# Up projection of the second block as seven products of halves, tokens stationary

## The reference, cut to what matters

```python
h = x + merged @ w_out
z = rmsnorm(h, norm_mlp) @ w_mlp_in              # 256 x 1024 by 1024 x 4096
return h + jnp.square(jax.nn.relu(z)) @ w_mlp_out   # 256 x 4096 by 4096 x 1024
```

## Time and profile before

| | us |
|---|---|
| median of 3 runs | 1961.76 (1961.75 to 1961.87) |
| the profiled execution, its own time | 1961.8 |
| its span, first to last instruction | 1960.0 |
| PE busy in the span | 1690.9 (86%) |
| up projection with `xtok` and `mean_mlp` | 113.15 (1747.29 to 1860.44) |
| down projection, PE's part | about 96.2 |

### The profile page before, as it was taken

The page is one execution under the profiler, slowest core; times in us unless marked ns, Lnnn a source line. Parts: engine busy times, 40 slices in busy tenths (PEclk is TensorE's granted clock), DMA queues, the critical chain, the costliest instruction groups (busy, mean ns, idle before and its releaser), DMA issues. The chain is left out here.

```text
span 1960.0 us, 21094 instructions
## 1 busy us (share of the span) xinstructions
PE 1690.9 (86%) x9114; PEld 1119.7 (57%) x9114; DVE 601.1 (31%) x1202; ACT 344.5 (18%) x735; POOL 0.2 (0%) x4
## 2 busy tenths in 40 slices
PE   9999985666676999999665766689999999999999
PEld 8788632222222887884221321258888888888844
DVE  4853210001000576431000000025567343210254
ACT  2241200000000322411000000012152344110000
POOL 0000000000000000000000000000000000000000
PEclk9999998788878999999888887899999999999999
DMA  8446899999999844389999999992433532334342
GB/s 358 162 170 277 350 427 429 434 429 429 432 430 427 338 161 155 148 346 412 428 431 433 425 434 429 429 417 107 152 132 118 171 106 94 129 129 171 134 174 100
DMA packets 31105, 561.45 MB, mean 286 GB/s; under 512 B 3584, under 2 KB 3840, under 8 KB 4992
## 3 DMA queue, kind: packets, MB, share of 16 engines
q1 hardware_dynamic: 31008, 560.03, 69.8%
HBM read 558.97 MB, written 1.05 MB: 286 GB/s over the span
## 5 line engine op out<-in xcount | busy, mean ns | idle before, releaser
L1797 PE MATMUL ps<-late,ring 128*128 128x256 f32 (+1 forms) x1312 | 286.7, 380 | 0.0
L1797 PEld LDWEIGHTS ps<-late,ring 128*128 128x128 f32 (+1 forms) x1312 | 244.7, 187 | 40.2 <-issue 3.3
L1345 PE MATMUL ps<-ring,hB 128*32 128x512 f32 x1024 | 155.6, 762 | 101.2 <-DMA ring<-in_stream 101.2
L660 PE MATMUL ps<-late,ring 128*128 128x256 f32 x1088 | 239.5, 380 | 0.0
L660 PEld LDWEIGHTS ps<-late,ring 128*128 128x128 f32 x1088 | 205.6, 190 | 31.1 <-issue 3.7
L1345 PE MATMUL ps<-l_extra,hB 128*32 128x512 f32 x768 | 114.9, 733 | 54.5 <-DMA l_extra<-in_stream 52.7
L1345 PEld LDWEIGHTS ps<-ring,hB 128*32 128x32 f32 x1024 | 41.2, 135 | 200.0 <-issue 199.1
L1357 PE MATMUL ps<-ring,hB 128*32 128x512 f32 x512 | 85.5, 825 | 63.1 <-DMA ring<-in_stream 63.0
L1345 PEld LDWEIGHTS ps<-l_extra,hB 128*32 128x32 f32 x768 | 28.6, 129 | 131.9 <-issue 129.1
L1103 DVE SCALAR_TENSOR_TENSOR l_extra<-l_extra,lpar 128x256 f32<-128x256 f32 x232 | 102.1, 482 | 3.6
L1455 DVE COPY hB<-ps 128x512 f32<-128x512 f32 x16 | 11.1, 692 | 284.9 <-PE ps L1357 284.9
(11 more groups left out here) (363 smaller groups left out, 1827.7 us busy)
## 6 DMA issues: line engine op xcount, KB each, us to landing
ring<-in_stream SPq DMA_DIRECT2D x40, 4096.0 KB, 52.4
ring<-in_stream SPq DMA_DIRECT2D x76, 2048.0 KB, 7.9
l_extra<-in_stream SPq DMA_DIRECT2D x26, 4096.0 KB, 53.1
l_extra<-in_stream SPq DMA_DIRECT2D x28, 2048.0 KB, 38.8
late<-in_stream SPq DMA_DIRECT2D x16, 2048.0 KB, 50.6
ring<-in_stream SPq DMA_DIRECT2D x6, 1792.0 KB, 19.4
ring<-in_stream SPq DMA_DIRECT2D x4, 1344.0 KB, 7.9
ring<-in_stream SPq DMA_DIRECT2D x2, 1764.0 KB, 9.9
```

The lines of the kernel that those rows point to most:

```text
L660: mm = self.nc.tensor.matmul(out[:, m * T:(m + 1) * T], w[:, k, c * P:(c + 1) * P], src[:, k, :], start=(k == 0), stop=(k == kc - 1))
L1345: mm = nc.tensor.matmul(out[js, :], x_slots[:, c, js], w[:, 0, j * D + at:j * D + at + FF], start=(c == 0), stop=(c == DC - 1))
L1797: mm = nc.tensor.matmul(out[0:width, m * T:(m + 1) * T], w[:, k, (c0 + m) * width:(c0 + m + 1) * width], src[:, k, :], start=(k == 0), sto ...
```

## The change

The up projection takes the scheme of the down projection. The 4096 output features are cut into four blocks `p` of 1024, and for each, the 256 tokens, the 1024 input features and the 1024 outputs into halves. Two slabs hold a block: `wa` the upper 512 input rows, `wb` the lower ones. Each of the seven products has 4 matmuls with a 128 by 128 piece of tokens (or token sums) stationary and 512 columns moving. So results lie with tokens on partitions, are combined by DVE from the banks into `tok`, and are turned back by transposes on PE (`turn`), 4 per quarter, 16 per block. ACT applies relu from the `turned` bank to `hidden`, and squares in place. DVE makes four token sums once, and four weight sums for each block, of 128 by 2048 each; two of them are written over the slabs. `xtok` has two banks instead of four, used twice. The last turn, of quarter 3 of block 3, stands behind the first product of the down projection, and the eight sums of down slab 0 are spread over block 3's gaps in DVE's program. The down projection is otherwise as it was.

```diff
-        s.add("mlp_in", second, P, DC, BANK)
+        s.add("mlp_in", second, P, DC // 2, D)
...
-    cols(np.asarray(a["w_mlp_in_2"][0]), 0, count=8)
+    up = np.asarray(a["w_mlp_in_2"][0])
+    for p in range(4):
+        for i in range(2):
+            put(chunked(up[BANK * i:BANK * (i + 1), D * p:D * (p + 1)]))
...
+    flat_bias = bias[:].rearrange("p h n -> p (h n)")
+    half_sums = "p (c n) -> p c n"
+    in_weight_sum = [[x.rearrange(half_sums, c=4) for x in pair_] for pair_ in ((region_c[:, 0:2048], region_g[:, 0:2048]), (flat_bias[:, 0:2048], flat_bias[:, 2048:4096]))]
+    in_token_sum = keep["late"][:, DC * T:].rearrange(four, a=4, c=4)
+    tok = sb("tok", [P, 4, BANK])
...
-                          ga=(6, 7, 6, 7), gb=(6, 7, 6, 7), y_a=(6, 7, 6, 7), y_b=(0, 1, 2, 3), w_out=(4, 5, 6, 7), mean_mlp=(0,),
-                          mlp_in=[1 + i % 3 for i in range(16)], xtok=(4, 5, 6, 7), product=(4, 5, 6, 7, 0, 2, 3)).items():
+                          ga=(6, 7, 6, 7), gb=(6, 7, 6, 7), y_a=(6, 7, 6, 7), y_b=(0, 1, 2, 3), w_out=(4, 5, 6, 7), mean_mlp=(7,),
+                          mlp_in=[i % 4 for i in range(28)], turned=[4 + i % 2 for i in range(16)], xtok=(6, 7, 6, 7),
+                          product=(6, 7, 0, 1, 2, 3, 4)).items():
         for i, b in enumerate(bs):
...
+            low, high = slice(0, 4), slice(4, 8)
+            def in_product(n, left, right):
+                out = claim("mlp_in", n)
+                for k in range(4):
+                    mm = nc.tensor.matmul(out[:], left[:, k], right[:, k], start=(k == 0), stop=(k == 3))
+                mm.then_inc(filled["mlp_in"], 1)
+            def turn(p, q):
+                out = claim("turned", 4 * p + q)
+                pe.wait_ge(tok_ready, 4 * p + q + 1)
                 for c in range(4):
-                    mm = nc.tensor.transpose(out[:, c * P:(c + 1) * P], xT[:, 4 * h + c, t * P:(t + 1) * P], ident)
-                mm.then_inc(filled["xtok"], 1)
-            fill("mlp_in", 1, w, 2, hA)
-            store.free(S_OF["mlp_in"], filled["mlp_in"], 2)
-            out = claim("mean_mlp", 0)
-            pe.wait_ge(sums["mlp"], 1)
-            for t in range(TT):
-                for c in range(2):
-                    mm = nc.tensor.matmul(out[:, t:t + 1], sq_mlp[:, c, t * P:(t + 1) * P], one[:, 0:1], start=(c == 0), stop=(c == 1))
-            mm.then_inc(filled["mean_mlp"], 1)
-            for i in range(1, 8):
-                project("mlp_in", i, 2 * i, hA)
+                    mm = nc.tensor.transpose(out[:, c * P:(c + 1) * P], tok[:, q, c * P:(c + 1) * P], ident)
+                mm.then_inc(filled["turned"], 1)
...
+            for p in range(4):
+                i = S_OF["mlp_in"] + 2 * p
+                wa, wb = store.wait(pe, i), store.wait(pe, i + 1)
+                xs, ws = in_token_sum, in_weight_sum[p % 2]
+                if p == 0:
+                    pe.wait_ge(scaled["mlp"], 4)
+                in_product(7 * p, hA[:, low, 0:P], wa[:, :, 0:BANK])
+                if p == 0:
+                    pe.wait_ge(scaled["mlp"], DC)
+                    token_copies()
+                pe.wait_ge(in_weight_sums, 4 * p + 2)
+                pe.wait_ge(in_token_sums, 1)
+                in_product(7 * p + 1, xs[:, 2], wa[:, :, BANK:])
+                store.free(i, filled["mlp_in"], 7 * p + 2)
+                if p:
+                    turn(p - 1, 3)
+                pe.wait_ge(in_weight_sums, 4 * p + 3)
+                pe.wait_ge(in_token_sums, 3)
+                in_product(7 * p + 2, xs[:, 1], ws[1])
+                in_product(7 * p + 3, hA[:, high, 0:P], wb[:, :, 0:BANK])
+                in_product(7 * p + 4, xs[:, 0], ws[0])
+                if p == 0:
+                    mean_tokens()
+                turn(p, 0)
+                pe.wait_ge(in_weight_sums, 4 * p + 4)
+                in_product(7 * p + 5, hA[:, high, P:], wb[:, :, 0:BANK])
+                turn(p, 1)
+                pe.wait_ge(in_token_sums, 4)
+                in_product(7 * p + 6, xs[:, 3], wb[:, :, BANK:])
+                store.free(i + 1, filled["mlp_in"], 7 * p + 7)
+                turn(p, 2)
...
-                pe.wait_ge(emptied["mlp_in"], 2 * s + 2)
+                pe.wait_ge(hidden_ready, 4 * (s // 2) + 3 + s % 2)
...
+                if s == 0:
+                    turn(3, 3)
...
+            def turned_out(p, q):
+                t, h = ((0, 0), (1, 1), (1, 0), (0, 1))[q]
+                act.wait_ge(filled["turned"], 4 * p + q + 1)
+                x = hidden(8 * p + 4 * h, 4).rearrange("p (c n) -> p c n", c=4)[:, :, t * P:(t + 1) * P]
+                sc_act(x, bank("turned", 4 * p + q)[:].rearrange("p (c n) -> p c n", c=4), ACT.Relu).then_inc(emptied["turned"], 1)
+                act.wait_ge(emptied["turned"], 4 * p + q + 1)
+                sc_act(x, x, ACT.Square).then_inc(hidden_ready, 1)
+            for p in range(4):
+                act.wait_ge(filled["mlp_in"], 7 * p + 1)
+                if p:
+                    act.wait_ge(emptied["mlp_in"], 7 * p)
+                nc.scalar.copy(first_product, bank("mlp_in", 7 * p)[:]).then_inc(emptied["mlp_in"], 1)
+                if p == 0:
+                    for b in range(4):
+                        act.wait_ge(filled["xtok"], b + 1)
+                        nc.scalar.copy(outtok[:, b // 2, b % 2 * BANK:(b % 2 + 1) * BANK], bank("xtok", b)[:]).then_inc(emptied["xtok"], 1)
+                else:
+                    turned_out(p - 1, 3)
+                for q in range(3):
+                    turned_out(p, q)
+            turned_out(3, 3)
...
+            def in_difference_1(p):
+                store.wait(dve, S_OF["mlp_in"] + 2 * p)
+                b11, b12, b21, b22 = in_weights(p)
+                vec.tensor_tensor(in_weight_sum[p % 2][0], b12, b11, ALU.subtract).then_inc(in_weight_sums, 1)
+            def in_difference_3(p):
+                store.wait(dve, S_OF["mlp_in"] + 2 * p + 1)
+                b11, b12, b21, b22 = in_weights(p)
+                dve.wait_ge(in_weight_sums, 4 * p + 1)
+                vec.tensor_tensor(b12, b22, b12, ALU.subtract).then_inc(in_weight_sums, 1)
+            def in_difference_2(p):
+                b11, b12, b21, b22 = in_weights(p)
+                t1, t2 = in_weight_sum[p % 2]
+                vec.tensor_tensor(t2, b22, t1, ALU.subtract).then_inc(in_weight_sums, 1)
+            def in_difference_4(p):
+                b11, b12, b21, b22 = in_weights(p)
+                dve.wait_ge(in_weight_sums, 4 * p + 3)
+                dve.wait_ge(filled["mlp_in"], 7 * p + 4)
+                vec.tensor_tensor(b21, b21, in_weight_sum[p % 2][1], ALU.subtract).then_inc(in_weight_sums, 1)
...
-                sum_bank("mlp", sq_mlp, b)
...
+                if b < 3:
+                    sum_bank("mlp", sq_mlp, b)
+                if b == 1:
+                    in_difference_1(0)
+                if b == 2:
+                    in_difference_3(0)
+            dve.wait_ge(scaled["mlp"], DC)
+            xs = in_token_sum
+            a11, a12, a21, a22 = hA[:, 0:4, 0:P], hA[:, 4:8, 0:P], hA[:, 0:4, P:], hA[:, 4:8, P:]
+            vec.tensor_tensor(xs[:, 2], a11, a21, ALU.subtract).then_inc(in_token_sums, 1)
+            vec.tensor_tensor(xs[:, 0], a21, a22, ALU.add).then_inc(in_token_sums, 1)
+            in_difference_2(0)
+            dve.wait_ge(in_token_sums, 2)
+            vec.tensor_tensor(xs[:, 1], xs[:, 0], a11, ALU.subtract).then_inc(in_token_sums, 1)
+            dve.wait_ge(in_token_sums, 3)
+            vec.tensor_tensor(xs[:, 3], a12, xs[:, 1], ALU.subtract).then_inc(in_token_sums, 1)
+            sum_bank("mlp", sq_mlp, 3)
+            for p in range(4):
+                n = 7 * p
+                dve.wait_ge(emptied["mlp_in"], n + 1)
+                dve.wait_ge(filled["mlp_in"], n + 3)
+                vec.tensor_tensor(second_u, bank("mlp_in", n + 2)[:], first_product, ALU.add).then_inc(second_ready, 1)
+                dve.wait_ge(second_ready, p + 1)
+                vec.tensor_tensor(third_u, bank("mlp_in", n + 1)[:], second_u, ALU.add).then_inc(emptied["mlp_in"], 2)
+                if p:
+                    dve.wait_ge(filled["turned"], 4 * p - 3)
+                dve.wait_ge(filled["mlp_in"], n + 4)
+                vec.tensor_tensor(tok[:, 0], bank("mlp_in", n + 3)[:], first_product, ALU.add).then_inc(emptied["mlp_in"], 1)
+                dve.wait_ge(emptied["mlp_in"], n + 4)
+                dve.sem_inc(tok_ready, 1)
+                in_difference_4(p)
+                if p:
+                    dve.wait_ge(filled["turned"], 4 * p)
+                dve.wait_ge(filled["mlp_in"], n + 5)
+                vec.tensor_tensor(tok[:, 1], bank("mlp_in", n + 4)[:], third_u, ALU.add).then_inc(tok_ready, 1)
+                step(vec.tensor_tensor(tok[:, 3], bank("mlp_in", n + 4)[:], second_u, ALU.add))
+                step.settle()
+                dve.sem_inc(emptied["mlp_in"], 1)
+                if p < 3:
```

(58 more changed lines are left out.)

67 lines of the change are left out of this document (30 added, 37 removed).

## The result

The changed kernel takes 1954.85 us (median of 7 runs, 1954.08 to 1957.4). The kernel before, beside it, took 1962.65 (7 runs, 1961.75 to 1963.72). The ratio is 0.9964, with a 95% interval of 0.9952 to 0.9975: faster by 0.36%, outside the 0.2% that I had set as the limit of what counts. The profiled execution took 1954.85 us, its span is 1953.1. The forecast was 1955.1, in a range of 1953.9 to 1957.8.

A forecast was written before the change was run, and what follows sets the result against it. PE bounds the up projection: 96.15 + 7.00 + 1.75 + 0.79 + 0.55 + 0.2 = 106.4 us instead of 113.15, 6.7 less than 1961.8, so 1955.1 us. Range 1953.9 to 1956.2 without, to 1957.8 with, late difference and most shape costs.

The forecast's parts named there:

- The bound: Up projection: PE is busy throughout, so time is the sum of its intervals, 106.4 us instead of 113.15.
- The 1.8 us around the span: Whole kernel: the profiled execution of before took 1961.8 us, its span 1960.0 with 1.8 around it.
- Products and turns: Up projection on PE: 112 matmuls at 0.8585, 96.15 us, and 64 transposes at 0.1094, 7.00 us.
- `xtok`: Start of the stage: PE waits for ACT's copy before reusing two banks, 0.55 us, bounds 0 and 1.0.
- Changes of shape: PE between matmuls and transposes, 32 changes: 0.2 us taken, range 0 to 3.2; rival with `xtok` at 1.0, 1958.6 us, 5%.
- The narrow edge: DVE's slab overwrite L2592 between products 3 and 5: needs 3.24 of 3.87 us, 0.63 remain; cost taken 0.
- The rival that I had left open: L2592 late in each block: PE waits 0.5 us four times, 1957.1 us, 10%.
- A transpose at its duration: Turns, groups of four between products, don't pipeline, each shows 272 ns: 10.4 us more, 1965.5 us, 5%.
- at a product's price per column: Turns: a transpose costs 0.2146 us, 6.7 us more, gain gone, 1961.8 us, 2%.

The follow-up runs named there:

- experiment 1: Changed kernel with every turn made twice into the same bank, 128 transposes of `tok` instead of 64: 1962.08 us, ratio to before 0.9997.
- experiment 5: Changed kernel without its 64 turns, ACT taking relu straight from `tok`, so the down projection gets untransposed numbers: 1948.45 us, ratio to before 0.9925.
- experiment 2: Changed kernel with `xtok` in four banks as before, instead of two used twice: 1955.26 us, ratio to before 0.9962.
- experiment 4: Changed kernel with three extra 128 by 512 DVE sums ahead of L2592 in each block: 1962.6 us; with one extra sum, 1957.47 us (single run).
- Experiment 6: Changed kernel's seven products with weights stationary and no turns, output complete: 1952.38 us, ratio 0.9947; with four `xtok` banks and a shorter mean, 1951.96 us.

## Why the prediction was right, point by point

- **The bound.** PE's sum of intervals was the right model: forecast 106.4 us for products, turns, `xT` and mean, measured 105.88 (1747.17 to 1853.05) and 0.44 for the last turn, 106.32. The 1.8 us around the span held.
- **The nearness of the time.** In part it is luck. I subtracted 6.7 us from 1961.8, but beside the changed kernel the kernel before took 1962.65, and the medians differ by 7.8 us, of which the stretch explains 6.84. The rest is of the size by which the stages ahead vary: the runs of the changed kernel alone range from 1954.08 to 1957.4. The 6.84 are the measured effect, not the 0.3 us between 1955.1 and 1954.85.
- **Products and turns.** 96.15 and 7.00 us stand in the trace to the hundredth: a block takes 25.79 us. The rows of the down projection and of L2048 had exactly the shapes that the change adds. Experiments 1 and 5 show both from the other side, 6.99 us for 64 transposes more, and 7.0 for 64 less.
- **`xtok`.** 0.55 forecast, 0.56 measured and taken back in experiment 2. It consists of a wait of 0.45 us and two restarts of 0.06 (the first transposes of the third and the fourth bank take 0.16 us instead of 0.11), so the second eight take 0.99 us for 0.87.
- **Changes of shape.** I took 0.2 of a range up to 3.2; it was 0 in blocks 1 to 3, and 0.07 is left of the 106.32 for all of the stage. The range rested on a misreading of the attention stage. The records beside the transposes took the steady 0.216 us there. The 0.1 us lie at the far ends of the two rows: the first record at 1567.99 took 0.32, behind matmuls of 64 rows, and the last before 1582.88 took 0.31, ahead of matmuls with 64 stationary columns.
- **The narrow edge.** The one poorly sized term, and its sum was off as well: 0.20 + 0.73 + 2.28 are 3.21 us, not 3.24. DVE's large instruction was right (2292 ns, estimated 2.28), but what comes ahead of it was not: the combination started 0.20 to 0.27 us behind PE, and after it DVE stood for 0.21 us, for its own write to be done and the semaphore to be raised, before L2592. The trace of DVE, block 1:

```profile
1790.12 0.69 DVE L2655 TENSOR_TENSOR b_tok<-ps,b_stat 128x512 f32<-128x512 f32 x1 [1.91 <-PE ps L2058]
1791.03 2.29 DVE L2592 TENSOR_TENSOR ring<-ring,b_bias 128x2048 f32<-128x2048 f32 x1 [0.21 <-DVE b_tok L2655]
1793.56 0.69 DVE L2662 TENSOR_TENSOR b_tok<-ps,b_rstd 128x512 f32<-128x512 f32 x1 [0.23 <-PE ps L2058]
```

  Product 4 starts at 1789.85, so the chain takes 3.47 us, not 3.24, and 0.40 us remain before product 5, not 0.63. With the weight load hidden I had 0.4; experiment 4 gives 0.25. It changed nothing, since that was enough. The rival that I had left open charged four blocks, and three could have paid: in block 0 the mean stands between the two products as well, and 1.32 us remain there. And PE does not read the slab while L2592 writes it: product 4 takes its weights from `b_bias` or `b_region_c`.
- **The rivals.** A transpose at its duration, or at a product's price per column: both refuted by experiment 1. The Trainium skill's figure of some 275 ns for a transpose, measured with bf16 ("TensorE: Matmul & The Clock Gate", section "Part 4: PE-mode transpose"), agrees with the duration here, 273 ns for L2066, and not with the price, 0.109. Its remark that transposes don't keep the clock up could not show here, where products stand between all groups: in experiment 1, with 128 of them, the granted clock is 1.00 from 1748.3 to 1860.7 us, and a product takes 3.43 us as before.
- **What I hadn't asked.** I took it as given that seven products need stationary tokens and turns. The row that would have raised the question was in the trace of before, a float32 matmul with 128 moving columns, (3.84 - 0.27) / 31 = 0.115 us a record:

```profile
1226.62 3.84 PE L1313 MATMUL ps<-l_work 128*128 128x128 f32 x32
```

  Experiment 6 shows that the way without turns is 2.9 us shorter.

## What to carry to other kernels

Where one engine has no gap, its time is the sum of intervals from start to start, and a change in its stage could be forecast here to a tenth of a microsecond from rows of the same shape (the time of the whole kernel varies by more); durations of pipelined instructions would have given the wrong sign here. Trading an eighth of the products for sums on an idle engine pays as long as each sum fits between the product that frees its operand and the product that wants it; look for that edge, count the wait for the engine's own write in it, and remember that whatever stands in it on the critical engine, such as a turn, is also cover. Before results are turned back, ask whether the other operand can be the stationary one, even if fewer columns move, down to the point where the weight loads set the pace.

## What the runs showed of the hardware that I had not expected

- A float32 matmul with a new 128 by 128 stationary piece and only 128 moving columns takes 0.2233 us (2 x 0.1117), against 0.4321 with 256 and 0.8585 with 512. A quarter of the last would be 0.2146. The mean's records, with one moving column, follow each other at 0.112 us too (L2082, eight in 0.81 us from 1766.65 to 1767.46, the first two 0.03 apart), and those of the kernel before with 30 columns as well (L1964, 32 in 3.49 us from 1553.94 to 1557.43, again the first two 0.03 apart):

```profile
1553.94 3.65 PE L1964 MATMUL ps<-b_kz,ring 128*128 128x30 f32 x32
1557.43 7.15 PE L1797 MATMUL ps<-late,ring 128*128 128x256 f32 x32
```

  So at 128 columns and below it is the weight load that sets the pace, one record in 0.112 us (a transpose in 0.109), although each load lasts 192 ns: fewer moving columns would save nothing more. The Trainium skill ("TensorE: Matmul & The Clock Gate", section "LDWEIGHTS (loading the stationary operand)") puts a load of 128 columns at 128 / 1.2, that is 107 ns. That lies near the interval, not the duration in the trace.
- PE starts a product 0.05 us after the end of the DVE instruction that it waited for (1797.48 to 1797.53), and its first record takes 0.53 us instead of 0.43, beside the wait itself. The first transpose after a wait takes 0.16 instead of 0.11.
- DVE's sums of 128 by 2048 took 2282 to 2293 ns beside a busy PE, over a slab or into a tile of their own. The one of experiment 4 in block 1, with PE idle for 1.5 us of it, took 2291: PE's work beside them did not lengthen them.
- The stages ahead, where PE waits for DMAs for over 200 us, end within 1.4 us of each other from profile to profile. An edit of half a microsecond at the end of such a kernel is visible in its own stretch, and not in the time.
